# A layer's lambda operations ahead of its norm, the raw tiles of layer 1 together, and the index search spread over more steps

## The reference, cut to what matters

```
def rms_norm(x, g):
    y = xf * lax.rsqrt(jnp.mean(xf * xf, axis=-1, keepdims=True) + EPS)
    return y * g
...
proj = rms_norm(h, g_mix_norm[i]) @ w_in
qa, ka, va, qi, ki, wi, qb, kb, vb, gate_a, gate_b = jnp.split(proj, ...)
lam = (jnp.exp(jnp.sum(lam_q1 * lam_k1)) - jnp.exp(jnp.sum(lam_q2 * lam_k2)) + lam_init)
...
# for each block of 128 queries
rel = jax.nn.relu(einsum('bthd,bsd->bths', qi, ki))
iscore = einsum('bths,bth->bts', rel, wi)
iscore = where(causal, iscore, -inf)
_, sel = lax.top_k(iscore, 128)          # k_top = min(256, 512 // 4)
# attention a reads only the selected keys, attention b all causal ones:
o_b = einsum('bhts,bshe->bthe', a1 - lam * a2, vb)
```

## Time and profile before

| what | value |
|---|---|
| median of 3 runs | 2711.01 us (2708.92 to 2717.32) |
| the profiled execution | 2721.82 us, its span 2720.5 us |
| mean granted clock of PE | 0.973 |
| PE busy | 2564.9 us, 94% of the span |
| DVE busy | 1536.6 us, 56% |
| ACT busy | 1101.7 us, 40% |
| POOL busy | 154.3 us, 6% |

### The profile page before, as it was taken

The page is one execution under the profiler, slowest core; times in us unless marked ns, Lnnn a source line. Parts: engine busy times, 40 slices in busy tenths (PEclk is TensorE's granted clock), DMA queues, the critical chain, the costliest instruction groups (busy, mean ns, idle before and its releaser), DMA issues.

```text
span 2720.5 us, 35826 instructions
## 1 busy us (share of the span) xinstructions
PE 2564.9 (94%) x14590; PEld 1909.7 (70%) x14590; DVE 1536.6 (56%) x2620; ACT 1101.7 (40%) x1736; POOL 154.3 (6%) x133
## 2 busy tenths in 40 slices
PE   6999999999998989999999999999999999999777
PEld 4677678888887777778888887766766658733226
DVE  5887556746557688555747475455544524422227
ACT  4436544433344435654424243354332323233235
POOL 1310000000000320000000000000000000022210
PEclk8999999999999999999999999999999989899998
DMA  4322233223222322232322232312111133699991
GB/s 154 116 82 86 85 128 101 93 95 105 91 97 78 114 93 91 88 118 100 107 94 93 95 106 79 126 43 88 48 50 44 43 110 126 249 380 399 403 373 69
DMA packets 70283, 342.97 MB, mean 126 GB/s; under 512 B 11618, under 2 KB 12514, under 8 KB 37220
## 3 DMA queue, kind: packets, MB, share of 16 engines
q1 hardware_dynamic: 64996, 332.22, 34.4%
q0 software_dynamic: 5120, 8.40, 0.9%
HBM read 312.26 MB, written 28.31 MB: 125 GB/s over the span
## 4 chain that ended last, share of the span: by engine, by line
PE 77%; DVE 9%; ACT 5%; SPq 4%; DMA 3%; issue 2%; POOLq 0%; DVEq 0%; ACTq 0%
PE bank L907 13%; PE bank L909 13%; PE bank L908 13%; PE bank L1127 4%; SPq L3527 4%; PE bank L1128 3%; PE bank L1129 3%; PE bank L3394 2%; PE bank L2497 2%; PE bank L1171 2%; DVE wl L1405 2%; ACT wh L2000 1%; PE bank L1201 1%; PE bank L1191 1%; DMA raw<-in_WE 1%
## 5 line engine op out<-in xcount | busy, mean ns | idle before, releaser
L1405 DVE TENSOR_TENSOR wl<-raw,wh 128x2048 fp32r<-128x2048 f32 (+1 forms) x165 | 370.5, 2247 | 160.8 <-ACT wh L2000 159.7
L907 PE MATMUL bank<-arena_rounded,wh 128*128 128x512 f32 x1056 | 413.1, 391 | 3.6 <-DVE arena_rounded L1665 3.2
L909 PE MATMUL bank<-arena_rounded,wl 128*128 128x512 f32 x1056 | 411.7, 390 | 0.0
L908 PE MATMUL bank<-arena_rounded,wh 128*128 128x512 f32 x1056 | 411.6, 390 | 0.0
L2000 ACT ACTIVATE wh<-raw 128x2048 fp32r<-128x2048 f32 (+1 forms) x165 | 303.3, 1840 | 167.2 <-DMA raw<-in_W 167.1
L907 PE MATMUL bank<-XH,wh 128*128 128x512 f32 (+1 forms) x728 | 292.5, 402 | 0.2 <-DVE XL L1704 0.2
L908 PE MATMUL bank<-XL,wh 128*128 128x512 f32 (+1 forms) x728 | 287.7, 395 | 0.0
L909 PE MATMUL bank<-XH,wl 128*128 128x512 f32 (+1 forms) x728 | 287.6, 395 | 0.0
L907 PEld LDWEIGHTS bank<-arena_rounded,wh 128*128 128x128 f32 x1056 | 198.7, 188 | 47.4 <-issue 5.1
L909 PEld LDWEIGHTS bank<-arena_rounded,wl 128*128 128x128 f32 x1056 | 198.6, 188 | 41.4
L908 PEld LDWEIGHTS bank<-arena_rounded,wh 128*128 128x128 f32 x1056 | 198.8, 188 | 41.0
(11 more groups left out here) (548 smaller groups left out, 4277.7 us busy)
## 6 DMA issues: line engine op xcount, KB each, us to landing
raw<-in_W SPq DMA_DIRECT2D x153, 1024.0 KB, 4.8
arena<-in_WE SPq DMA_DIRECT2D x31, 1024.0 KB
wh_full<-in_WE SPq DMA_DIRECT2D x15, 1024.0 KB
raw<-in_WE SPq DMA_DIRECT2D x15, 1024.0 KB
gsave<-scr SPq DMA_DIRECT2D x48, 256.0 KB
scr<-gsave SPq DMA_DIRECT2D x48, 256.0 KB, 4.0
XH_full<-in_WE SPq DMA_DIRECT2D x10, 1024.0 KB
XL_full<-in_WE SPq DMA_DIRECT2D x10, 1024.0 KB
```

Of the source, the lines that this page charges most:

```text
L907: pe.matmul(ps[0:c.stop - c.start, :], h[:, k, c], hi, start=i == 0, stop=False)
L908: pe.matmul(ps[0:c.stop - c.start, :], h[:, k, c], lo, start=False, stop=False)
L909: mm = pe.matmul(ps[0:c.stop - c.start, :], l[:, k, c], hi, start=False, stop=i == len(xs) - 1)
L1405: w_lo.inc(dve.tensor_tensor(wl[:, i % 3, 0:k], raw[:, i % 3, 0:k], wh[:, i % 3, 0:k].bitcast(F32), ALU.subtract), i)
```

## The change

On DVE, the three operations on the lambdas' parameters move from the start of `first_projections` to the start of `rms`, and the raw heads 0 and 1 leave the loop over k: all three follow it. On PE, layer 1 runs the three raw tiles together over k (it waits for blocks n0 and n0 + 1 first), with the sums behind k = 1 and the spread behind k = 2, where they were behind k = 3 and k = 5 of a loop over two tiles; layer 0 keeps its tile 2 apart, with the spread behind its step 0 instead of 3. The search makes 5 moves in steps 7 to 12, 4 in 13 to 18 and 2 in 19 (56 in all), and in attention 1 in steps 1 to 11 and 24 to 38, 2 in steps 12 to 23, the rest in 39, again none in a step with a cut. At the first head of a query tile of kind a DVE waits for its own last signalled result.

```
--- before
+++ after
@@ raw_projections (PE)
-                keys = [("win", li, i) for i in range(2)]
-                split(n0)
+                keys = [("win", li, i) for i in range(3 if li else 2)]
+                split(n0 + 1 if li else n0)
                 ps = [opened(key) for key in keys]
-                h, l = weights(n0, 256)
+                w = [weights(n0 + i // 2, 256) for i in range(3)]
                 for k, hi, lo in xs:
                     pe.wait_ge(*x((("raw", r), k)))
                     for i, key in enumerate(keys):
-                        c = slice(128 * i, 128 * i + 128)
+                        c = slice(128 * (i % 2), 128 * (i % 2) + 128)
+                        h, l = w[i]
...
-                    if li and k == 3:
+                    if li and k < KT - 1:
+                        raw_used.inc(mm, (r, k))
+                    if li and k == 1:
                         norm_sums(r)
-                    if li and k == 5:
+                    if li and k == 2:
                         norm_row(r)
                 if li == 0:
                     pe.wait_ge(c_first, 16)
                     norm_sums(r)
-                split(n0 + 1)
-                tile(("win", li, 2), weights(n0 + 1, 256), slice(0, 128), xs, None, {} if li else {3: lambda: norm_row(r)},
-                     lambda mm, k: raw_used.inc(mm, (r, k)))
+                    split(n0 + 1)
+                    tile(("win", li, 2), w[2], slice(0, 128), xs, None, {0: lambda: norm_row(r)},
+                         lambda mm, k: raw_used.inc(mm, (r, k)))
@@ rms (DVE)
                 r = 3 * li
+                v.inc(dve.tensor_scalar(tz(22 + li), K(f"gsub{li}", 0), 1.0 - lam_init(li), None, ALU.mult))
+                dve.tensor_tensor(tz(16), K(f"lam{li}", 0), K(f"lam{li}", 1), ALU.mult)
+                lam_m.inc(dve.tensor_tensor(tz(17), K(f"lam{li}", 2), K(f"lam{li}", 3), ALU.mult), li)
                 norm_row(r, WROW)
...
-                    if k in (4, 5):
-                        raw_head(li, k - 4)
-                raw_head(li, 2)
+                for s in range(3):
+                    raw_head(li, s)
@@ first_projections (DVE)
-                dve.wait_ge(s_in, 16)
                 dve.wait_ge(c_in, 16)
-                v.inc(dve.tensor_scalar(tz(22 + li), K(f"gsub{li}", 0), 1.0 - lam_init(li), None, ALU.mult))
-                dve.tensor_tensor(tz(16), K(f"lam{li}", 0), K(f"lam{li}", 1), ALU.mult)
-                lam_m.inc(dve.tensor_tensor(tz(17), K(f"lam{li}", 2), K(f"lam{li}", 3), ALU.mult), li)
...
                     if 7 <= s < 20:
-                        for _ in range(8 if s < 13 else 5 if s < 18 else 2):
+                        for _ in range(5 if s < 13 else 4 if s < 19 else 2):
                             next(pick, None)
@@ attention (DVE)
                             if kind == "a" and ti == 0 and h == 0:
                                 dve.wait_ge(*hrec((m, 3)))
+                            elif kind == "a" and h == 0:
+                                dve.wait_ge(*v())
...
-                        if s < 15:
-                            for _ in range(0 if s == 0 or cuts_at(m, s - 1) else 3):
+                        if s < 39:
+                            for _ in range(0 if s == 0 or cuts_at(m, s - 1) else 2 if 12 <= s < 24 else 1):
                                 next(pick, None)
-                        elif s == 15:
+                        elif s == 39:
                             for _ in pick:
                                 pass
```

## The result

Over five runs each the kernel before took 2712.25 us (2708.92 to 2717.75) and the changed kernel 2700.24 (2700.03 to 2703.93). The ratio is 0.9948, with a 95% interval from 0.9936 to 0.9959: 11 to 17 us faster. The forecast was 2679, with a range from 2667 to 2698. So the sign was right, but more than half of the 32.2 us is missing. The profiled execution after took 2703.93 (span 2702.6); that of before, on which the sum was made, had taken 2721.82, some 10 us over its own median. Among the executions of the kernel before that go with the experiments, all six above 2719 us have a mean granted clock of 0.972 to 0.974, and all but one of the thirteen under 2715 us have 0.975 to 0.977; the profiled one has 0.973. Between the two traces 17.9 us can be followed. That is itself more than the medians show.

What follows compares the result with a forecast made beforehand. PE was taken as bound by waits for DVE, with half clock behind some. Gains of 17.7 us (layer 0) and 14.5 (layer 1), together 32.2, off the median 2711.0 gave 2678.8; forecast 2679, range 2667 to 2698.

Steps and rivals of the forecast that it cites:

- The projections' term: Projections: fewer search moves remove waits for heads and at attention's start, gaining 14.0 us in layer 0, 11.8 in layer 1.
- Rival (a): Half of the projections' gain is caught by ACT, POOL or the cuts: 12.9 us less, 2692; chance 0.15.
- (c): DVE's backlog in attention never clears; 35 moves of steps 12 to 39 cost 26.6 us a layer: 2726; chance 0.04.
- (d): Early parts give their upper bounds and attention loses nothing: 2668 us; chance 0.13.
- (e): Nothing measurable: later heads and layer 1's later start use up the lambdas' gain, ACT next; within 8 us; chance 0.04.
- (b): All twenty moves of attention's steps 12 to 23 lie on the path: 15.2 us a layer, 2703; chance 0.08.
- the two signs of being wrong: Projections keep a DVE wait over 3 us after step 6, or attention loses over 8 us in a layer.
- the start of the layers: Earlier lambdas, raw heads moved: 3.0 us gained in layer 0 (bounds 1, 5.4), 2.0 in layer 1 (-1.5, 4).
- Rope 1 ends at 51.2: Layer 0: cut of block 3, behind rope 1, lets projection 4 start at 54.4; PE waits 4 to 5 us.
- attention's loss: Attention's steps 12 to 23, two moves each: 3.0 us lost a layer, bounds 0 and 7.6; net +0.7 with earlier gains.
- 22.8 of 20.9: Attention's steps 16 to 23: DVE's 12.2 us busy plus 10.6 for 14 moves, against the 20.9 us PE needs.
- The reference point: Whole kernel: 32.2 us off the profiled 2721.8 gives 2689.6; the same gain off the median 2711.0 gives 2678.8.

Runs made afterwards that it cites:

- Experiment 4: Changed kernel with the cut of block n0 + 3 in DVE's step 1, ahead of rope 0: 2690.38 us, 0.9904 of the kernel before.
- experiment 3: Changed kernel with attention's moves two in each of steps 1 to 11, one in steps 12 to 38: 2696.41 us, 0.993 of the kernel before.
- experiment 5: Changed kernel with both the cut of block n0 + 3 ahead of rope 0 and attention's moves shifted early: 2680.78 us, 0.9875 of the kernel before.
- experiment 7: Changed kernel without the 43 search moves of each attention: 2686.14 us, 0.9889 of the kernel before.
- search only: Kernel before with only the new distribution of search moves, old lambdas, heads and raw tiles: 2703.27 us, 0.9957 of the kernel before.
- moves early: Same kernel as experiment 3: changed kernel with attention's moves two a step up to step 11, then one: 2696.41 us.
- cut first: Same kernel as Experiment 4: changed kernel with the cut of block n0 + 3 ahead of rope 0: 2690.38 us.
- head only: Changed kernel with the old distribution of search moves, keeping the new lambdas, raw heads, spread and raw tiles: 2711.21 us, 0.9986 of the kernel before.

## Why the prediction was right and wrong

**Right.** The projections' term was 14.0 us for layer 0: the lead goes from 1.4 at 100 us to 16.0 at 190, so 14.6, and no spread of a head is waited for. For layer 1, 11.8 were forecast and 11.0 measured (11.3 to 22.3 behind attention's first steps). The score wait of step 10 went with its slow clock: +3.8 and +3.5 for a forecast 3.7. The new wait of 2.8 us at layer 1's raw tiles came as 2.73, and the last normed tile of layer 1 at 866.3, that is 877.8 in the time of the kernel before, for 877.7. Rival (a) fell, for the projections' gain is whole; (c), (d) and (e) fell with the time. The result lies between what (a) and (b) gave and nearer to (b), whose mechanism holds in part: the moves of steps 12 to 23 cost 6.5 us of the 15.2 that it asked for. Neither of the two signs of being wrong that I had named appeared, so they were set too wide to catch what failed.

**Wrong: the start of the layers, 5.0 forecast and about 1.2 measured.** The step that failed is "Rope 1 ends at 51.2, the cut, 3.4 us long beside POOL, at 54.4". I gave the cut its price beside POOL and the two ropes their price without it, 0.7. They have two SBUF inputs and run beside POOL as well: 1.76 and 1.74. Rope 1 ended at 52.4 and the cut at 55.65, and PE's wait ahead of projection 4 was 6.95 us and not 4 to 5. The price stood in the trace of the kernel before, in a row that I hadn't used, where two ropes beside POOL take 1.7 us each:

```profile
47.51 3.46 DVE L1606 TENSOR_TENSOR arena<-arena,scr 128x512 f32<-128x512 f32 x2
```

Of the 1.6 us missing in layer 0, rope 1 is 1.0 and POOL's end 0.1 (the sum's own terms, 51.2 + 3.4, give 54.6), and 0.4 is the slow clock. The rule that I had cited for one operation, from the Trainium skill, page "SBUF — State Buffer", section "SBUF: two separate sides", holds for each: whoever starts first keeps the shared port pair "for the whole instruction; the other fully blocks". The runs agree, by the three ends that lie 0.55, 0.55 and 2.15 us behind the ends of POOL's instructions. The price of the slow clock behind the wait was nearly right in size (projection 4's tile took 8.2 us at a granted clock of 0.69 instead of 5.4, so 2.8 more; 2.4 was forecast). In layer 1 the same happened: ropes of 1.79 and 1.73, a cut of 3.35 that ended at 881.40, a wait of 5.27, and a slow tile. The change of lead there is -0.2 instead of +2.0. That 2.0 was also more than its own terms gave: projection 4 at 891.5 to 892 instead of 895.5, less 2.4, is 1.1 to 1.6. Experiment 4 shows what this order is worth: with the cut ahead of the first rope, layer 0's start leads by 4.6 us more (5.8 if both leads are counted from 28 us), and layer 1's gives 7.3 where it gave -0.2.

**Wrong: attention's loss, 3.0 a layer forecast, 6.5 and 6.3 measured.** The step that failed is "22.8 of 20.9 ... PE slips some 2.5 us at step 22". The working shown counts DVE's busy time against PE's; of the handovers that I say I followed it shows none. DVE's work and ACT's form a ring instead: the score goes to ACT, its sum comes back for the probability, PE transposes it, ACT copies it. Two moves at 0.7 us sit between two handovers, and the moves can't slide into the idle time elsewhere, since DVE keeps its order; it idles for 5.8 of 26.4 us. The second part is the clock, which I priced at nothing here: behind the waits at 248.5 and 252.9 the 8 us from 252 on have a granted clock of 0.79. At full rate these would be at most 1.7 us shorter, by my estimate from 8 x 0.21. One move a step (experiment 3) puts the stretch at 22.1 us, at clock 1.00:

```profile
240.56:262.68 22.12, 20.90 (x129) 16.33 (x128) 16.44 (x55) 15.40 (x37) 0.00 (x0) 1.00 0.28 97
```

The ten extra moves of steps 12 to 23 cost less elsewhere: experiment 3 has eight of them in steps 1 to 11 and two in step 39, and pays 2.0 us for it, by the lead at step 12.

**Not foreseen: 1.8 and 2.1 us behind attention.** The first matmuls of the branches run at half clock in the changed kernel's trace. The four us from their start (first row), and those of experiment 5 (second fence):

```profile
333.40:337.40 4.00, 4.00 (x11) 3.17 (x12) 0.00 (x0) 2.51 (x5) 0.00 (x0) 0.57 0.21 79
```

```profile
325.10:329.10 4.00, 4.00 (x18) 3.29 (x19) 0.69 (x1) 2.48 (x5) 0.00 (x0) 1.00 0.20 74
```

Eleven matmuls against eighteen. The wait ahead of them, 1.6 us, is the same in both. It isn't the moves': experiment 7 has none and shows the same at 0.61, and loses 1.2 there; search only, moves early and cut first have full clock at this place. In layer 1 again five kernels and the changed one lose between 0.7 and 2.8 us behind attention, and three lose next to nothing. Why the clock falls in some traces and not in others at a place with the same work isn't settled. One trace a kernel can't tell a chance of one execution from a property of the kernel.

**The reference point.** The 32.2 us were taken from the profiled execution and moved unchanged to the median, "so the same gain gives 2678.8". The traces differ by 17.9 us, the medians by 12.0, so 5.9 of what is missing lies here and in no wait. The half-clock spells that I counted as gains are no chance of that one execution: head only, with the old schedule, has them behind a wait for the heads' spread and at attention's start as well, and search only, with the old head, has those behind the lambda waits. Where else the execution of before lost its 10 us isn't known.

In sum, over both layers and against the forecast: the starts -3.8, the projections -0.2 (14.6 and 11.0 for 14.0 and 11.8), attention -6.9 (3.8 - 6.5 and 3.5 - 6.3 for twice +0.7), behind attention -3.9. That is 14.8 less than 32.2: 17.4, which is the lead at 1227 us. The rest of the program adds 0.5 to make the 17.9 of the traces.

## What to carry to other kernels

When work is moved to where another engine shares a port, give every operation there its contended price, not only the one that was already seen beside it, and look first whether the one that others wait for can go ahead of the contention. Free time on an engine is worth only as much as lies between two handovers: fillers of 1.4 us ahead of a 0.3 us operation delay a whole ring of engines, and one at a time costs a fifth to two fifths of what pairs cost (over steps 16 to 23, 1.1 us in experiment 3 and 2.2 in experiment 5, against 5.4). A profile-based gain in which clock spells are counted should be held against the median with a discount.

## What the runs showed of the hardware

DVE's two-input operations beside POOL end 0.55 us (128 x 512) and 2.15 us (128 x 2048) behind the end of the POOL operation that was running, in all three cases of layer 0 and within 0.01 us in those of layer 1: in both layers such a rope takes 1.73 to 1.79 us instead of 0.68, and 3.35 instead of 2.29. When DVE is first it is POOL that is slow: POOL's second operation of a head takes 1.71 where it runs into a rope and 1.29 where it doesn't, and in experiment 4 its first one takes 1.90, issued while the cut runs, for 1.28.

The granted clock can differ at one place between kernels with the same work and the same wait ahead of it: 0.57 and 0.61 in two traces and 1.00 in four, at the first matmuls behind attention of layer 0, worth 1.6 us each.
